# A decode stage that loads two paged caches: the second cache's page loads are asked for by GpSimd instead of the sync engine

## What is computed

```python
past = (cache_a_kv[l][page_table].reshape(db, past_len, 2, H_A, HEAD),
        cache_b_kv[l][page_table].reshape(db, past_len, 4, DH_B), ...)
...
s = jnp.einsum('bqhcd,bkhcd->bchqk', qb, kf) * scale      # A: two maps per head, w = p0 - lam * p1
return jnp.einsum('bhqk,bkhv->bqhv', w, vf)
...
ss = jnp.einsum('bqhd,bqnpd->bqhnp', qf, kg) * scale      # B: blocks of 64 rows picked by top-k
o_sel = jnp.einsum('bqhk,bqkd->bqhd', ps, vg)
```

## Time and profile before

| | us |
|---|---|
| median of three runs | 1792.59 |
| lowest and highest | 1791.8 and 1804.48 |
| the profiled execution | 1781.35 |
| its span, first to last instruction | 1778.6 |
| decode stage in it | about 1022 to 1530 |

### The profile page before, as it was taken

One profiled execution on the slowest core, in us unless ns is written; L12 is line 12 of the kernel. 1 busy time (PEld: TensorE's weight loads), 2 busy tenths in 40 slices (PEclk: granted clock), 3 DMA queues, 4 the chain that ended last, 5 costly groups with the idle time before them and its releaser, 6 DMA issues. The chain is left out here.

```text
span 1778.6 us, 39060 instructions
## 1 busy us (share of the span) xinstructions
PE 1623.3 (91%) x14840; PEld 1257.1 (71%) x14840; DVE 788.8 (44%) x1554; ACT 612.8 (34%) x1410; POOL 138.5 (8%) x219
## 2 busy tenths in 40 slices
PE   7999999998899889998996788889989889789998
PEld 6888888877678767776765566666666667567776
DVE  5222121254138444344335345665666565773321
ACT  4311121242013313312204345555555555642210
POOL 3000000044100010000003000000000000110010
PEclk9999999999899999998998799999999999899999
DMA  7565565586633234337235679899889879763455
GB/s 232 158 193 190 176 199 146 195 287 220 213 113 107 72 109 132 113 107 207 89 95 208 245 283 379 322 346 357 331 320 364 298 279 358 265 219 105 158 177 168
DMA packets 219160, 379.58 MB, mean 213 GB/s; under 512 B 42301, under 2 KB 122206, under 8 KB 218174
## 3 DMA queue, kind: packets, MB, share of 16 engines
q1 hardware_dynamic: 210462, 350.38, 58.1%
q0 software_dynamic: 7520, 24.09, 4.0%
q10 hardware_dynamic: 992, 2.62, 0.4%
HBM read 344.47 MB, written 40.71 MB: 217 GB/s over the span
## 5 line engine op out<-in xcount | busy, mean ns | idle before, releaser
L372 PE MATMUL pj_ps<-pj_whi,pj_xhi 128*128 128x512 f32 (+1 forms) x1024 | 415.1, 405 | 7.8 <-PEq L95 6.0
L373 PE MATMUL pj_ps<-pj_wlo,pj_xhi 128*128 128x512 f32 (+1 forms) x1024 | 400.3, 391 | 0.0
L374 PE MATMUL pj_ps<-pj_whi,pj_xlo 128*128 128x512 f32 (+1 forms) x1024 | 399.0, 390 | 0.0
L297 DVE TENSOR_TENSOR pj_wlo<-pj_w,pj_whi 128x1024 fp32r<-128x1024 f32 (+1 forms) x128 | 156.9, 1227 | 443.2 <-ACT pj_whi L255 442.0
L255 ACT ACTIVATE pj_whi<-pj_w 128x1024 fp32r<-128x1024 f32 (+1 forms) x128 | 132.2, 1033 | 502.9 <-DMA pj_w<-in_w_in 502.9
L372 PEld LDWEIGHTS pj_ps<-pj_whi,pj_xhi 128*128 128x128 f32 x1024 | 196.3, 192 | 67.7 <-issue 31.6
L374 PEld LDWEIGHTS pj_ps<-pj_whi,pj_xlo 128*128 128x128 f32 x1024 | 196.5, 192 | 40.2
L373 PEld LDWEIGHTS pj_ps<-pj_wlo,pj_xhi 128*128 128x128 f32 x1024 | 196.8, 192 | 33.8
L1904 ACT ACTIVATE fr_kT<-da_tp 128x512 f32<-128x512 f32 x200 | 119.5, 597 | 164.0 <-PE da_tp L1778 161.1
L2014 DVE COPY fr_kT<-da_tp 128x512 f32<-128x512 f32 x128 | 88.4, 691 | 83.0 <-PE da_tp L1778 82.9
L1778 PE MATMUL da_tp<-all_ident,fr_front 128*128 128x128 f32 x640 | 95.5, 288 | 22.0 <-DMA fr_front<-in_cache_a_kv 12.2
(11 more groups left out here) (566 smaller groups left out, 2159.9 us busy)
## 6 DMA issues: line engine op xcount, KB each, us to landing
fr_front<-in_cache_a_kv SPq DMA_DIRECT2D x128, 512.0 KB, 6.3
da_pa<-in_cache_a_kv SPq DMA_DIRECT2D x128, 512.0 KB, 6.0
pj_w<-in_w_in SPq DMA_DIRECT2D x119, 512.0 KB, 4.6
px_pages<-in_cache_b_kv SPq DMA_DIRECT2D x256, 128.0 KB, 2.4
fr_front<-in_cache_b_kv SPq DMA_DIRECT2D x128, 128.0 KB, 6.6
da_pb<-in_cache_b_kv SPq DMA_DIRECT2D x128, 128.0 KB, 6.1
proj<-pj_out SPq DMA_DIRECT2D x52, 256.0 KB, 5.3
fr_kT<-in_w_out SPq DMA_DIRECT2D x16, 512.0 KB, 4.8
```

The lines of the kernel that those rows point to most:

```text
L297: dve.tensor_tensor(self.wlo[:, r, :, 0:n], self.w[:, r, :, 0:n], self.whi[:, r, :, 0:n], ALU.subtract).then_inc(self.wlo_ready, 1)
L372: pe.matmul(acc, hi, high, start=kc == 0, stop=False)
L373: pe.matmul(acc, hi, low, start=False, stop=False)
L374: last = pe.matmul(acc, lo, high, start=False, stop=kc == KC - 1)
```

## The change

`load_group` is split into `load_a`, which SP keeps, and `load_b`. For the first four groups (m < 4) SP still issues both. From group 4 on POOL issues B: it reads the four page numbers into registers of its own, waits for the same value of `summed` as SP, and raises semaphores of its own, `later_b_loaded`, for which PE waits. POOL's program is now a loop over the steps in which the load of B stands ahead of the guest's turns of that step.

```diff
-def load_group(nc, d, k, sp, m, a, b, wait=None):
-
-    _, pages = nc.values_load_multi_w_load_instructions(
-        k.page_rows[0:1, 4 * m:4 * m + 4], engines=[mybir.EngineType.SP],
-        min_val=0, max_val=d.cache_b.shape[0] - 1)
+def page_ids(nc, d, k, engine, m):
+
+    return nc.values_load_multi_w_load_instructions(
+        k.page_rows[0:1, 4 * m:4 * m + 4], engines=[engine],
+        min_val=0, max_val=d.cache_b.shape[0] - 1)[1]
+
+def load_a(nc, d, k, sp, m, a, wait=None):
+
+    pages = page_ids(nc, d, k, mybir.EngineType.SP, m)
     if wait is not None:
         sp.wait_ge(*wait)
     for i in range(4):
         sp.dma_start(a[:, i, :], d.cache_a[bass.ds(pages[i], 1), :, :]
                      .rearrange("a p n -> p (a n)")).then_inc(k.a_loaded[m % RING], 16)
+
+def load_b(nc, d, k, eng, engine, m, b, loaded, wait=None):
+
+    pages = page_ids(nc, d, k, engine, m)
+    if wait is not None:
+        eng.wait_ge(*wait)
     for i in range(4):
-        sp.dma_start(b[:, i, :], d.cache_b[bass.ds(pages[i], 1), :, 256:512]
-                     .rearrange("a p n -> p (a n)")).then_inc(k.b_loaded[m % RING], 16)
+        eng.dma_start(b[:, i, :], d.cache_b[bass.ds(pages[i], 1), :, 256:512]
+                      .rearrange("a p n -> p (a n)")).then_inc(loaded[m % RING], 16)
...
-                    load_group(nc, d, k, sp, m, k.early_a[m], k.early_b[m])
+                    load_a(nc, d, k, sp, m, k.early_a[m])
+                    load_b(nc, d, k, sp, mybir.EngineType.SP, m, k.early_b[m], k.b_loaded)
...
+        later_b_loaded = s.sems("later_b_loaded", RING)
...
-                        load_group(nc, d, k, sp, m, pa[m % RING], pb[m % RING], (summed, old) if old else None)
+                        load_a(nc, d, k, sp, m, pa[m % RING], (summed, page_step[m - RING] + 1) if m >= RING else None)
+                        if m < RING:
+                            load_b(nc, d, k, sp, mybir.EngineType.SP, m, pb[m], b_loaded)
...
             @block.gpsimd
             def _(pool):
-                for _ in guest.pool(pool):
+                tiles = guest.pool(pool)
+                for n in range(N + 2):
+                    if n >= 2 and n - 2 in page_step:
+                        m = page_step.index(n - 2) + RING
+                        if m < DB * NG:
+                            load_b(nc, d, k, pool, mybir.EngineType.Pool, m, pb[m % RING], later_b_loaded, (summed, n - 1))
+                    for _ in range(guest.turns_of(n, N) if guest.FROM <= n < N else 0):
+                        next(tiles, None)
+                for _ in tiles:
                     pass
...
-                        pe.wait_ge((b_loaded if j else a_loaded)[m % RING], 64 * (m // RING + 1))
+                        if j == 0:
+                            pe.wait_ge(a_loaded[m % RING], 64 * (m // RING + 1))
+                        elif m < RING:
+                            pe.wait_ge(b_loaded[m], 64)
+                        else:
+                            pe.wait_ge(later_b_loaded[m % RING], 64 * (m // RING))
```

More of the change, by code:

```diff
@@ L1640, in decode_attend @@
     a_of = {n: a for a, n in enumerate(a_steps)}
+    page_step = [n for n in range(N) if steps[n][1] == "page"]
     tp_order = []
@@ L1719, in _ @@
                             continue
-                        old = next((x + 1 for x in range(N) if steps[x][1] == "page"
-                                    and steps[x][0] * NG + steps[x][2] == m - RING), None)
-                        load_group(nc, d, k, sp, m, pa[m % RING], pb[m % RING], (summed, old) if old else None)
+                        load_a(nc, d, k, sp, m, pa[m % RING], (summed, page_step[m - RING] + 1) if m >= RING else None)
+                        if m < RING:
+                            load_b(nc, d, k, sp, mybir.EngineType.SP, m, pb[m], b_loaded)
                     elif what == "win":
```

## The result

The changed kernel is slower: 1808.09 us in the median against 1791.72 us, and the ratio of the two is 1.0121 with a 95% interval of 1.0099 to 1.0142, which is 17.7 to 25.4 us and in the middle 21.7. I had forecast 1801.7 us, 9.1 us of loss. The direction is that of the forecast and so is the mechanism of its one costly term, which was less than half of what was lost; two terms were missing. Ratios here compare undisturbed executions alone; one profiled execution, that of the kernel with B ahead of A on SP, was a disturbed one with a low clock.

A forecast was written before the change was run, and what follows sets the result against it. The prediction took PE's chain in decode as the bound, with transfers close beside it. Seven borders x 1.3 us = 9.1 us, added to the timed 1792.59 us, gave 1801.7 us, range 1787 to 1818.

The forecast's parts named there:

- the sum: Decode stage: 7 borders between batches, each shifted once by 1.3 us, make 9.1 us; all other parts 0.
- PE's chain and the 12 us of waits: Decode stage: PE sets the pace; transfers win only in 9 waits for A pages at batch borders, 12.2 us.
- SP loses B, saving 0: SP's issue: 60 groups of four B loads leave, but SP was late only where pages had room; saving 0.
- POOL gains B, cost 0: POOL in decode: register reads and four issues take 3.8 us a group against about 6.7 available; cost 0.
- the third rival, a slow requester: POOL needs 8.2 us a group instead of 3.8 and asks for border B pages late: 1819 us, chance 0.15.
- B takes A's place on the engines, 1.3 us a border: DMA engines at batch borders: about 0.9 of B's packets go ahead of A's last, delaying A by 1.3 us.
- my bound of 1.5: Upper bound in us on A's delay at a border, with all of B ahead of A's last packet.
- the two delays don't add up: At a border, the first two groups' loads are both delayed 1.3 us, but the border shifts by 1.3 us once.
- queue 0 yields: Rival on the DMA queues: B's packets come through only when A's are done; price 0, 1792.6 us, chance 0.15.
- two queues fill the engines better: Rival on the DMA engines: both queues move 390 GB/s, so A lands earlier and nearly all waits go; 1781 us, chance 0.10.
- 30,000 more packets in queue 0: Sign that the forecast is right: POOL's DMA queue would carry about 30,000 more packets.

The follow-up runs named there:

- key-split kernels on SP alone: Kernel before, but SP loads A's key halves, then B, then A's value halves: all groups 1.0041; first two groups of each batch 0.997; first group alone 1.0095.
- the kernel with the filler: Changed kernel plus twelve identity transposes on PE ahead of its wait for A at the first group of every border: 1.0102 against the kernel before.

## Why the forecast was right and wrong

The step that failed is the sum: its one term above nothing was too small (9.1 us for what measured 13.3 us of waits), and two losses stood in it at nothing, the lower clock behind the longer waits (some 5.4 us) and GpSimd's longer drain at the stage's exit (4.0 us).

*PE's chain and the 12 us of waits.* Right: what was lost in the stage is in L1806's waits for A and in the clock behind them, and taking half of A out of their way at the borders gained 0.3%.

*SP loses B, saving 0.* Right: where SP lost three quarters of B and the borders kept theirs, PE's waits stayed at 13.3 us. The key-split kernels on SP alone show the converse, that SP counts as soon as it issues twelve loads a group.

*POOL gains B, cost 0.* Right for its pace: 2.32 us of issues and 1.38 us of register reads are 3.7 us a group, I had 3.8, and PE never waited for B; the third rival, a slow requester, falls. Wrong for its end: I put the whole term at 0 and didn't cost POOL's drain at the stage's exit, 4.0 us.

*B takes A's place on the engines, 1.3 us a border.* The mechanism was right (the later landings of an A that was asked for as before, the runs with the borders alone and without B), the size was not: 9.1 us of waits forecast, 13.3 measured. The mean from first issue to last landing went from 8.8 to 10.4 us at p0 and from 9.3 to 11.0 at p1: 1.6 and 1.7, above even my bound of 1.5, where I had counted only a group's own B and a share of 0.9 of it. And "the two delays don't add up" failed in part: at four borders (groups 8, 24, 32, 40) PE now waits at p0 and again at p1, before at two. The waits grew by 13.3 us, 1.9 a border. One B ahead of A is worth 1.4 us of that; that the rest comes of p1's A standing behind p0's later one is argued and not shown, though the border at 1190 us, where p1 alone pays, speaks for it.

*Left out.* These two terms were at nothing without a reason given: the lower clock behind long waits, some 5 us in the profiled run, and the exit's 4.0. With them 13.3 + 5.4 + 4.0 = 22.7 us by the two profiled executions, beside 21.7 by the medians. The 5.4 is a remainder; that the kernel with the filler took 6.0 us less from B turn to B turn, with waits and fillers together only 1.7 us below the changed kernel's waits, bears it out in the main.

The rival "queue 0 yields" falls by A's later landings, "two queues fill the engines better" too: with B on POOL, A took longer at 13 of the 14 border loads, and at the one left (p0 of group 24, with B 4 us behind) 9.4 us against 9.7. Of the signs I named, 30,000 more packets in queue 0 were 11,520 (7,520 before): 240 loads went as 48 packets each, where SP's queue, with 34,560 fewer, had needed 144. For these 31.5 MB queue 0's share of the span, in time, grew by 88 us (4.0% of 1778.6 us to 8.8% of 1803.3) and queue 1's fell by 92 (58.1% to 52.2%), so the packets of POOL's queue were no dearer; it was their place that cost.

## What to carry to other kernels

A second issuing engine does not add bandwidth: ask which load ends last at each place, and what comes in front of its last packet, in whichever queue or beside it. Splitting a load by when its parts are wanted gained where the issuing engine had time for it, and lost where it didn't, or where the next load was left whole and the wait moved on to it. When an engine takes up DMA work, look at the stage's exit as well as at its pace, and price a long wait (the clock fell behind 32 of the 43 waits of 2 us and over here) with what the lower clock adds behind it.

## What was unexpected of the hardware

- GpSimd's drain before a barrier ended 1.1 us behind the engine's last addition without page loads of its own and 1.5 to 7.8 us behind it with them, by no rule of number or time that the runs show.
- The clock fell to 1.2 GHz behind waits of 3.0, 3.1 and 4.1 us, and the matmuls behind it took 1.8 times as long (2.07 against 1.12 us). Over all kernels but one it did so behind 15 of 16 waits of 3 us and over, and 17 of 27 of 2 to 3 us. It did not behind a wait of 3.67 us (group 56), and it fell once, in the kernel with the filler, where PE had not just waited, so the wait's length alone does not decide. The Trainium skill, TensorE: Matmul & The Clock Gate, section "Part 1: The HAM clock gate", has the clock follow how busy the array has been of late; these rows agree in kind.
- A load asked for by GpSimd 0.5 us behind A delayed A by 1.6 us; the one asked for 4 us behind did not delay that A (9.4 against 9.7 us), but the next was 1.9 us later.
